# w_down of both feed-forward steps: sixteen of twenty-two K tiles in one split of seven block products, six tiles plain

## The reference

```python
def swiglu_ffn(x, w_gate_up, w_down):
    g, u = jnp.split(x @ w_gate_up, 2, axis=-1)
    return (jax.nn.silu(g) * u) @ w_down

r = x + 0.5 * rms_norm(swiglu_ffn(rms_norm(x, norm_ffn1_pre), w_ffn1_gate_up, w_ffn1_down), norm_ffn1_post)
z = rms_norm(r, norm_mix_pre) @ w_in                   # attention and short convolution follow
r = r + rms_norm(mixed, norm_mix_post)
r = r + 0.5 * rms_norm(swiglu_ffn(rms_norm(r, norm_ffn2_pre), w_ffn2_gate_up, w_ffn2_down), norm_ffn2_post)
gate = jax.nn.sigmoid(rms_norm(r, norm_ple_pre) @ w_ple_gate)
r = r + rms_norm(gate * (p @ w_ple_proj), norm_ple_post)
```

## Time and profile before

| | us |
|---|---|
| median of 3 runs | 1043.55 (1042.89 to 1043.71) |
| the profiled execution's own time | 1043.57 |
| its span in the trace | 1041.8 |
| TensorE busy | 1021.6 |
| VectorE busy | 778.3 |
| ScalarE busy | 531.9 |
| GpSimd busy | 289.5 |

### The profile page before, as it was taken

One profiled execution on the slowest core, in us unless ns is written; L12 is line 12 of the kernel. 1 busy time (PEld: TensorE's weight loads), 2 busy tenths in 40 slices (PEclk: granted clock), 3 DMA queues, 4 the chain that ended last, 5 costly groups with the idle time before them and its releaser, 6 DMA issues.

```text
span 1041.8 us, 20086 instructions
## 1 busy us (share of the span) xinstructions
PE 1021.6 (98%) x8019; PEld 1003.6 (96%) x8019; DVE 778.3 (75%) x1183; ACT 531.9 (51%) x955; POOL 289.5 (28%) x224
## 2 busy tenths in 40 slices
PE   7999999999999999999999999999999999999997
PEld 7999999999999998999999999999999999999897
DVE  5899877878885369678695898977777888438843
ACT  5645555555733354434555555555555654227664
POOL 3212444343120343000323201343434221134221
PEclk9999999999999999999999999999999999999999
DMA  8313443334145321331334121443434334433002
GB/s 235 94 47 92 112 120 85 108 96 137 46 117 148 75 43 51 82 89 50 73 82 121 42 81 42 122 121 82 121 82 115 109 81 112 112 102 98 26 2 86
DMA packets 179740, 94.84 MB, mean 91 GB/s; under 512 B 11896, under 2 KB 177984, under 8 KB 179648
## 3 DMA queue, kind: packets, MB, share of 16 engines
q1 hardware_dynamic: 179632, 93.56, 32.8%
q10 hardware_dynamic: 16, 0.00, 0.0%
HBM read 91.15 MB, written 2.50 MB: 90 GB/s over the span
## 4 chain that ended last, share of the span: by engine, by line
PE 83%; DVE 12%; issue 2%; ACT 1%; DMA 1%; SPq 1%; POOL 0%; POOLq 0%; DVEq 0%; ACTq 0%
PE bank L2110 11%; PE bank L2111 10%; PE bank L2112 10%; PE bank L2239 8%; PE bank L2241 8%; PE bank L2242 8%; PE bank L2159 5%; PE bank L2336 2%; PE bank L2333 2%; PE bank L2335 2%; PE bank L2167 2%; PE misc L2357 2%; PE misc L2239 1%; PE misc L2241 1%; PE misc L2242 1%
## 5 line engine op out<-in xcount | busy, mean ns | idle before, releaser
L768 POOL TENSOR_TENSOR s_rest<-s,raw_up 128x512 f32<-128x512 f32 x38 | 82.9, 2181 | 294.8 <-DVE s L1460 294.8
L741 POOL TENSOR_TENSOR ssq<-ssq,sq 128x272 f32<-128x272 f32 x99 | 93.2, 941 | 120.8 <-ACT sq L830 114.5
L2239 PE MATMUL bank<-t_hi,even_blocks 128*128 128x272 f32 x432 | 124.9, 289 | 0.0
L2241 PE MATMUL bank<-t_lo,even_blocks 128*128 128x272 f32 x432 | 124.8, 289 | 0.0
L2242 PE MATMUL bank<-t_hi,even_blocks 128*128 128x272 f32 x432 | 124.8, 289 | 0.0
L2239 PE MATMUL bank<-t_hi,odd_blocks 128*128 128x272 f32 x384 | 111.3, 290 | 0.9 <-ACT kept L904 0.8
L2241 PE MATMUL bank<-t_lo,odd_blocks 128*128 128x272 f32 x384 | 111.0, 289 | 0.0
L2242 PE MATMUL bank<-t_hi,odd_blocks 128*128 128x272 f32 x384 | 110.9, 289 | 0.0
L2111 PE MATMUL bank<-x_lo,w_split 128*128 128x272 f32 x320 | 92.1, 288 | 0.0
L2239 PEld LDWEIGHTS bank<-t_hi,even_blocks 128*128 128x128 f32 x432 | 81.4, 188 | 0.1
L2242 PEld LDWEIGHTS bank<-t_hi,even_blocks 128*128 128x128 f32 x432 | 81.3, 188 | 0.0
(11 more groups left out here) (365 smaller groups left out, 3345.0 us busy)
## 6 DMA issues: line engine op xcount, KB each, us to landing
raw_up<-w_ffn_gate_up SPq DMA_DIRECT2D x88, 512.0 KB, 5.1
raw<-w_ffn_down SPq DMA_DIRECT2D x16, 704.0 KB, 5.7
raw_up<-w_ffn_down SPq DMA_DIRECT2D x16, 512.0 KB, 4.9
raw<-w_in SPq DMA_DIRECT2D x14, 512.0 KB, 3.9
raw<-w_ple_gate SPq DMA_DIRECT2D x8, 512.0 KB, 3.9
ca_raw<-w_ffn_down SPq DMA_DIRECT2D x8, 384.0 KB, 4.6
x_tok<-x_prompt SPq DMA_DIRECT2D x4, 512.0 KB, 5.3
raw<-w_in SPq DMA_DIRECT2D x8, 256.0 KB, 4.7
```

The source lines that it names most:

```text
L741: nc.gpsimd.tensor_tensor(dst, dst, sq[:, s % 2, :], ALU.add).then_inc(summed, 1)
L768: nc.gpsimd.tensor_tensor(s24(j)[:, 0, :], s31[:, 1, :], a[:, 0, :], ALU.add).then_inc(s24_made[n], 1)
L2239: nc.tensor.matmul(out, hi[:, k, :], x_h, start=(k == 0 and p in (1, 2, 7)), stop=False, skip_group_check=True)
L2241: nc.tensor.matmul(out, hi[:, k, :], x_l, start=False, stop=False, skip_group_check=True)
```

## The change

w_down's three parts go. K tiles 0 to 15 are one split of seven: a block is 8 K tiles of one output tile, and each product p runs over all four pairs i of output tiles before the next p begins. K tiles 16 to 21 are plain. TensorE's order is: product 1 (i = 0 to 3), product 2, the plain units of the even output tiles (A and B), products 6, 7, 5, 4, the plain units of the odd output tiles, product 3. A product unit has 24 matmuls, a plain unit 18.

Weights are now loaded by quadrant: quad q is 8 K tiles of all four even (q = 0, 1) or odd (q = 2, 3) output tiles, 4 x 512 KB. The low part of a weight overwrites its raw form in place, so that quads 0 and 1, which are used alone (products 1 and 2) and in sums, are loaded a second time. All sums of weights (`quad_sum`, 16 a stage) are made by DVE; POOL makes none here. `even_a`, `even_b`, `odd_a`, `odd_b` and `make_c22` put the outputs together. The first four weight chunks of the next stage are loaded once the odd plain units of half B are done. In ple, `turn_r(1)` is issued after the two `lo_pass` calls of half B instead of before them. In mix, the sum of A's r squares moves from mix's first units into product 3, that of B's y squares to step 6 of the first pass.

```diff
+    HK, CT, NP = KD, KF - 2 * KD, KD // 2
+    WIDE = [(p, i) for p in (1, 2, 6, 7, 5, 4, 3) for i in range(NP)]
+    PLAIN = [("even", i, h) for g in (0, 2) for h in (A, B) for i in (g, g + 1)] + \
+            [("odd", i, h) for h in (A, B) for i in range(NP)]
...
+            def load_down(n, d):
+                sp.wait_ge(block_lo_made[n], 4 * NJ)
+                load_quads(d, 0)
+                sp.wait_ge(product_done[n], len(SEVEN))
+                load_quads(d, 1)
+                sp.wait_ge(up_a_made[n], NJ)
+                load_quads(d, 2)
+                load_plain(d, "even", 2), load_plain(d, "even", 3)
+                sp.wait_ge(tokens_summed, 5 * (n + 1))
+                load_plain(d, "even", 0), load_plain(d, "even", 1)
+                sp.wait_ge(product_done[n], wide(1, NP - 1))
+                load_quads(d, 0)
+                load_quads(d, 3)
+                sp.wait_ge(product_done[n], wide(2, NP - 1))
+                load_quads(d, 1)
+                sp.wait_ge(product_done[n], wide(7, NP - 1))
+                for i in range(NP):
+                    load_plain(d, "odd", i)
...
+            def quad_sum(n, kind, i):
...
+                if kind == "s0":
+                    dve.wait_ge(quad_in[0], 16 * NP * (2 * n + 2))
+                    dve.wait_ge(quad_in[2], 16 * NP * (n + 1))
+                    dst, x, y = a0, a0, a2
+                if kind == "x":
+                    dve.wait_ge(quad_in[3], 16 * NP * (n + 1))
...
+                    dst, x, y = sum_x(i), a0, a3
+                if kind == "s3":
+                    dve.wait_ge(quad_in[1], 16 * NP * (2 * n + 2))
...
+            def wide_jobs(n, s):
...
+                even_a(n, s, 0), even_a(n, s, 1)
+                quad_sum(n, "s0", 0), quad_sum(n, "x", 0)
+                weights_low(n, ("even", 3))
+                quad_sum(n, "s0", 1), quad_sum(n, "x", 1)
+                even_a(n, s, 2)
+                quad_sum(n, "s3", 0)
+                weights_low(n, (6, 0))
+                even_a(n, s, 3)
+                quad_sum(n, "s3", 1)
+                weights_low(n, (6, 1))
+                quad_sum(n, "s0", 2), quad_sum(n, "x", 2), quad_sum(n, "s3", 2)
...
             def down_stage(s, ci):
...
+                wide_jobs(n, s)
+                odd_b(n, s, 0)
+                chain_r(ci, A, y_down, SUM0[s], {0: lambda: odd_b(n, s, 1), 2: lambda: odd_b(n, s, 2), 5: lambda: odd_b(n, s, 3)})
                 split_lo(c1)
...
+                even_b(n, s, 0)
                 if with_p:
                     p_lo(0)
...
+                chain_lo(ci, A, range(0, 3))
+                split_lo(c1 + 1)
...
+            def plain_products(n, s, kind, i, h, hooks={}):
...
+                if kind == "even" and h == B:
+                    pe.wait_ge(y_ready, Y0[s] + i + 1)
...
+            def down_stage(s, n, turns=None):
+
+                n0 = SUM0[s]
+                wide_products(n, 1)
+                wide_products(n, 2)
+                for kind, i, h in PLAIN[0:2 * NP]:
+                    plain_products(n, s, kind, i, h)
+                for p in (6, 7, 5, 4):
+                    wide_products(n, p)
+                for kind, i, h in PLAIN[2 * NP:]:
+                    plain_products(n, s, kind, i, h, {CT - 1: lambda: all_sums(n0)} if (i, h) == (0, B) else {})
+
+                def turn_tokens():
+                    pe.wait_ge(y_ready, Y0[s] + 3 * NP)
+                    turns()
+                wide_products(n, 3, {1: {4: turn_tokens} if turns else {}, 3: {2: lambda: all_sums(n0 + 1)}})
...
                     if h == B:
                         add_square(OWN_SUMS[1], KD - 1)
-                        turn_r(1)
                     for n, (u, c, _) in enumerate(gates):
                         lo_pass(u, c, lambda k, h: x_low(3, k, h), h, None if n else lambda k: pe.wait_ge(x_ready, 48 + 8 * h + k + 1))
+                    if h == B:
+                        turn_r(1)
```

More of the change, by code:

```diff
@@ L57, in encoder_layer @@
     NJ = KF - NCL
[L61 to L65, removed]
+    STAGES = [("up1", 2 * KF, 4 * NCL, KD), ("down1", 0, 2 * KD, 0), ("mix", len(MIX), 2 * len(MIX), KD),
+              ("out", KD, 2 * KD, KD), ("up2", 2 * KF, 4 * NCL, KD), ("down2", 0, 2 * KD, 0),
               ("ple", KD, 4 * KD, KD + KP)]
@@ L370, in ca_bank @@
[L370 to L383, removed]
@@ L619, in load_up, with load_quads, load_plain @@
                     sp.dma_start(raw_up[:, slot_of[c]], up[s][j % 2, j // 2]).then_inc(w_loaded[slot_of[c]], 16)
[L621 to L638, removed]
+            def load_quads(d, q):
+                half, odd = q % 2, q // 2
+                for i in range(NP):
+                    sp.dma_start(quad(quads, q, i), w_down[d][2 * i + odd][:, half * HK:(half + 1) * HK]).then_inc(quad_in[q], 16)
+            def load_plain(d, kind, i):
+                sp.dma_start(weights_at((kind, i), False), w_down[d][2 * i + (kind == "odd")][:, 2 * HK:KF])\
+                    .then_inc(plain_in[i], 16)
+            def load_down(n, d):
[14 more added lines that the diff above has]
+                sp.wait_ge(product_done[n], wide(7, NP - 1))
+                for i in range(NP):
+                    load_plain(d, "odd", i)
             def load_short(cs):
@@ L699, in _ @@
             load_short(range(C0["ple"], C0["ple"] + SLOTS))
-            sp.wait_ge(unit_done, U0["ple"] - 4)
+            sp.wait_ge(unit_done, plain("down2", "odd", NP - 1, A))
             sp.dma_start(p_tok[:, 0:XT - 1, 0:KP * P], t["p_prompt"][0, 0].rearrange("(i p) n -> p i n", p=P))\
@@ L952, in jobs, with even_b_copy, square_y @@
+            def even_b_copy(n, i):
+                act.wait_ge(unit_done, plain(("down1", "down2")[n], "even", i, B))
+                nc.scalar.activation(y_down(2 * i, B), other_bank(i), ACT.Copy).then_inc(even_b_copied, 1)
+            def square_y(s, v):
+                act.wait_ge(y_ready, Y0[s] + v + 1)
+                square(y_down(2 * (v % NP) + (v // NP in (1, 2)), v // KD), SQ0[s] + v + (KD if v >= KD else 0)).then_inc(squared, 1)
             def jobs(n, s):
@@ new lines, in weights_low @@
+            def weights_low(n, *bs):
+                for b in bs:
+                    dve.wait_ge(weights_hi_made, weights_no(n, b))
+                    nc.vector.tensor_tensor(weights_at(b, True), weights_at(b, False), weights_hi(b).bitcast(F32), ALU.subtract)\
+                        .then_inc(weights_lo_made, 1)
+            def quad_sum(n, kind, i):
+                s = ("down1", "down2")[n]
+                a0, a1, a2, a3 = (quad(quads, q, i) for q in range(4))
+                if kind == "s0":
[4 more added lines that the diff above has]
+                    dve.wait_ge(quad_in[3], 16 * NP * (n + 1))
+                    dve.wait_ge(quad_summed, qsum_no(n, "s0", i))
+                    if i:
+                        dve.wait_ge(unit_done, plain(s, "even", i - 1 if i < 3 else 3, B))
+                    dst, x, y = sum_x(i), a0, a3
+                if kind == "s3":
+                    dve.wait_ge(quad_in[1], 16 * NP * (2 * n + 2))
+                    dve.wait_ge(quad_summed, qsum_no(n, "x", i))
+                    dst, x, y = a1, sum_x(i), a1
+                if kind == "s1":
+                    dst, x, y = a2, a2, a3
+                nc.vector.tensor_tensor(dst, x, y, ALU.add).then_inc(quad_summed, 1)
```

767 lines of the change are left out of this document (370 added, 397 removed).

## The result

The changed kernel takes **1054.74 us** (median of 4 runs, 1053.27 to 1056.33) against 1043.63 for the kernel before on the same chip (1042.89 to 1043.88): ratio 1.0111, 95% interval 1.0098 to 1.0123. I had predicted 1044, range 1036 to 1051. The profiled execution has 1056.33 of its own, 1.6 above the median, a span of 1054.5, and a mean granted clock of 0.987.

A forecast was written before the change was run, and what follows sets the result against it. The prediction took the kernel to be bound by the number of matmuls on TensorE. From 1043.6 us, 17.1 saved and 17.8 lost gave 1044.3, predicted as 1044, no measurable change, range 1036 to 1051.

The forecast's parts named there:

- matmuls saved: On TensorE, each w_down goes from 1008 to 960 matmuls; 96 saved at 0.126 us, 12.1 us less.
- waits that go: TensorE's waits at the first plain tiles 0.6, into mix 1.3, into ple 1.6, at turn_r 1.5 us would go.
- first load and `keep_u4`: End of up: quad 0's load and the keep_u4 copy just fit; counted nothing, up to 1.4 us for both stages.
- transfers: In w_down, 12.06 MB at 300 GB/s make even unit (3, B) 5.0 us late, 10.0 us for both stages.
- clock behind these waits: Behind the transfer waits in both w_down stages, the forecast counted no loss from a lowered clock.
- VectorE behind them: After (3, B), VectorE owes twelve operations until product 6's fourth block; 2.0 us for both stages (0 to 3).
- A's squares: The sum of A's squares, 1.9 us behind the last odd A unit, needs 2.3 us; 0.8 us for both stages.
- sum in mix: After product 3, B's last add stands behind a reciprocal on VectorE, making mix's sum late; 1.0 us (0 to 2).
- p: In down2, p's load takes 8.2 us behind ple's chunks, TensorE wants it after 6.8; 1.4 us (0 to 3).
- sum in ple: p_lo(0) waits for p's turn and ScalarE, delaying B's adds and the next sum; 2.6 us (0 to 4).
- next late behind `turn_r`: In ple, once turn_r(1)'s 1.5 us wait is covered, nothing else would be late; 0 us.
- rival of the clock: Waits pull the clock down: at 289 GB/s each stage has one over 3 us, 1.6 us each, 1050.5; chance 0.20.

The follow-up runs named there:

- turn_again: The same kernel as turn_only, run again because that run's profiled execution couldn't be used; 1042.76 us.
- turn_only: The kernel before with only turn_r(1) moved behind the low matmuls of ple's first group B; 1043.11 us.
- no_second: The changed kernel without the second loads of quads 0 and 1, their sums made from quads already there (output not the reference's); 1038.71 us.
- warm: The changed kernel with 36 idle turns on TensorE in front of even unit (3, A) (output not the reference's); 1056.38 us.
- ends: The changed kernel with p loaded before ple's first four chunks and the last even B add before a chunk's low weights and the reciprocal; 1051.12 us.
- turn_tg: turn_only with the low weights of ple's chunks 4 to 7 put behind the next group's tG on VectorE; 1041.86 us.
- q3_early: The changed kernel with three of quad 3's four tiles (1.57 MB) asked for in up's last job, behind quad 0; 1043.60 us.
- reload_rows: The changed kernel with second loads of quads 0 and 1 reading 4 KB rows of x_prompt, same size (output not the reference's); 1047.20 us.

## Why the prediction was wrong

| step | predicted, us | the profile of after |
|---|---|---|
| matmuls saved | -12.1 | x7923, -12.1 |
| waits that go (`ca_w_lo`, mix, ple, `turn_r`) | -5.0 | -4.8: they are gone, 0.2 left in mix |
| first load and `keep_u4` | 0 (to 1.4) | 0.5 and 0.2 |
| transfers | 10.0 | waits for them: 0.59 + 4.87 + 0.48 + 4.18 = 10.1 |
| clock behind these waits | 0 (rival 3.2) | 2.7 and 3.3 |
| VectorE behind them | 2.0 | 2 x (1.1 + 0.2) = 2.5 |
| A's squares | 0.8 | 0 |
| sum in mix | 1.0 | 2.25, and 1.6 for the clock |
| p | 1.4 | 2.4 |
| sum in ple | 2.6 | 1.8 |
| next late behind `turn_r` | 0 | 1.0 |

The terms of the last column give +11.5; the profiled executions differ by 12.8, so 1.3 us of small gaps have no name here.

**The step that failed is the clock**, which I had put at nothing and which makes 7.6 us of the last column. Behind the wait of 3.11 us in the earlier trace rows the granted clock stands at 0.50. I took the length of that one wait for the point from which the clock falls, which no trace had shown, and sized the new waits at 2 and 2.6 us, short of it. On paper already the second size was wrong: by the prediction's own terms (3, A), due at 296.1, waits until 298.0 (quad 3 at 295.9, a sum of 1.2 and a low part of 0.95), which is 1.9 us, and of the 5.0 us in all 3.1 are left for (3, B), not 2.6. At its central rate the forecast stood on its own point.

In the runs three things failed. First, the wait was not two such pieces. Quad 3 landed at 300.7 and not at 295.9, so all of it fell on (3, A): 4.9 and 4.2 us, over the point that I had set. The burst began at about 262.5, with `keep_u4` late and 1.1 us to the first byte, and moved 12.06 MB in 43 us, 279 GB/s (287 in down2, from 836 to 878), below the 293 at which, by my terms, one wait would come to 3.11 us. In down2 its windows hold 282 to 305 GB/s from 838 to 860, in down1 they dip to 233 to 254 from 276 to 282; no run says why. And when quad 3 had landed, 10.6 MB had moved where the loads up to it are 9.96: the loads behind were taking their share.

Second, the point itself was wrong. From one row I had made a threshold; the profiles of the thirteen kernels (turn_again for turn_only) show, behind 255 us, 35 waits of TensorE of 0.9 to 1.5 us and no fall of the clock behind any, 23 waits of 1.5 to 2.7 us with a fall behind 11, and 8 of 3.1 us or more with a fall behind all.

Third, its price was low. The rival's 1.6 us a fall, taken twice, were my estimate from the start of the program, where the clock stood at 0.62, 0.50, 0.50 and 0.67 in the four windows from 14 to 18 us; no run shows them as the price of a new wait. Behind (3, A) matmuls worth 15.9 us (126 at 0.126) took 18.5 and 19.2 us, and there was a third fall, behind the sum in mix: from that sum to the 0.6 us wait for `w_split` in front of 424.38 there are 24.2 us in the kernel after and 22.6 in no_second, whose clock stayed up, the same instructions. How much of the first two is the clock's alone isn't settled: warm shows that the second quad 1 would have taken part of it.

A fall can also cost nothing. From the turn of p to the sum in ple there are 14.1 us in after, where the clock stays up and the sum waits 1.8 us, and 14.0 in no_second, where the clock falls and the sum waits 0.2: the slow matmuls filled the wait that came next.

**The transfers** came out at their size, 10.1 for 10.0, but by luck: the rate was too high (300 for 279 and 287, though 289 was my lower bound, and the steady windows of full load say 290 to 295), and the distribution over the places wrong. The chance for the rival of the clock, 0.20, was too small because I put the mean of a few spiky microseconds where a burst of 40 us was to be priced.

**The ends.** Mix's sum was mis-sized, 2.25 for 1.0: I had counted the reciprocal ahead of the add and not the chunk's low weights, which also stand there (ends took the wait away by moving the add before both):

```profile
394.35 1.44 DVE L1428 TENSOR_TENSOR w_split<-raw,w_split 128x1024 fp32r<-128x1024 f32 x1
395.72 1.84 DVE L1434 RECIPROCAL rpre<-misc 128x272 f32<-128x272 f32 x1
397.60 0.44 DVE L1704 TENSOR_TENSOR h_raw<-bank,h_raw 128x272 f32<-128x272 f32 x1
```

For p it was 2.4 for 1.4: from the issue of ple's third chunk (952.0) to p's landing (961.0) it took 9.0 us and not 8.2, and TensorE came as reckoned. **turn_r**: "next late there is nothing" was wrong, tG was next late; turn_only, turn_again and turn_tg show it.

**What held**: the count of matmuls and their price, the place of the waits, VectorE's debt in product 6, no waits in products 5 and 4, that the split itself is worth its 12 us. Two of the signs of being wrong came up, the clock under 0.9 behind 306 us (0.56 there) and the wait for `keep_u4` (0.5 us). The chances have a slip: by their own terms they are faster 0.41, same 0.23, slower 0.36.

## What to carry to other kernels

A transfer-bound stretch is priced at the rate of the steady full windows of the same source (w_down here: 290 to 295 GB/s), and a load in it lands later than its own bytes would have it (quad 3 when 10.6 MB had moved, not 9.96); before such a burst look for microseconds in which the queue is idle and a place already free, since 1.57 MB asked for before the burst and not in it were worth 11 us here. A wait of TensorE of about 2 us can cost more than its 2 us: in 11 of 23 cases here the clock fell behind it, which was 1.6 more in mix, and nothing behind p, where another wait came next. By these counts several waits under 1.5 us should be cheaper than one of their sum; no run tested that. When an edit takes a wait away, look on every engine for what comes next in that place: of the 1.5 us of `turn_r` only a second edit, on another engine, brought the larger part.

## What I had not expected of the hardware

The clock fell behind idle stretches of TensorE as short as 1.75 us in one place (q3_early, (3, B)) and stayed up behind 2.6 in another (warm, the turn of p). That a kernel's runs spread over 3 to 5 us (1053.3 to 1056.3; q3_early 1041.2 to 1046.0) where the kernel before spreads over 1 to 2 (2.0 in 21 runs) fits this, but wasn't tested. And one queue moved 399 to 410 GB/s (reload_rows) from rows of 4 KB, between stretches of 290 to 295 from w_down's runs of 512 bytes.
